# Two levels of a gated recurrence: the same score blocks from narrower matmuls

## The reference, cut to what matters

```
def step(state, xs):
    qc, kc, vc, gc = xs
    cum = jnp.cumsum(gc, axis=2)
    o_inter = jnp.einsum('bhtk,bhkv->bhtv', qc * jnp.exp(cum), state)
    rel = jnp.where(tri[:, :, None], cum[:, :, :, None, :] - cum[:, :, None, :, :], -jnp.inf)
    scores = jnp.einsum('bhtk,bhsk,bhtsk->bhts', qc, kc, jnp.exp(rel))
    o_intra = jnp.einsum('bhts,bhsv->bhtv', scores, vc)
    ...
```

## Time and profile before

| | |
|---|---|
| median of 3 runs | 2507.85 us (2505.35 to 2508.05) |
| the profiled execution, its own time | 2508.06 us |
| its span, first to last instruction | 2506.3 us |
| mean granted TensorE clock | 0.994 |
| TensorE matmul busy | 2473.7 us, 99% |
| TensorE weight loads busy | 2067.1 us, 82% |
| VectorE busy | 1455.4 us, 58% |
| ScalarE busy | 1251.8 us, 50% |

### The profile page before, as it was taken

The page is one execution under the profiler, slowest core; times in us unless marked ns, Lnnn a source line. Parts: engine busy times, 40 slices in busy tenths (PEclk is TensorE's granted clock), DMA queues, the critical chain, the costliest instruction groups (busy, mean ns, idle before and its releaser), DMA issues.

```text
span 2506.3 us, 32631 instructions
## 1 busy us (share of the span) xinstructions
PE 2473.7 (99%) x11947; PEld 2067.1 (82%) x11947; DVE 1455.4 (58%) x1732; ACT 1251.8 (50%) x1604; POOL 44.9 (2%) x103
## 2 busy tenths in 40 slices
PE   8999999999999999999999999999999999999997
PEld 7888878888888888888888888878888888888886
DVE  6479665545445454445566566566666666544465
ACT  5357744444444444444654355456556555444464
POOL 2300000000000000000000000000000000000000
PEclk9999999999999999999999999999999999999999
DMA  7543445666666666555654555555565656665554
GB/s 254 175 134 113 135 136 184 191 187 191 186 191 188 189 192 202 192 192 178 171 175 135 151 143 177 186 158 183 186 185 183 190 178 189 199 200 193 193 194 142
DMA packets 234754, 446.27 MB, mean 178 GB/s; under 512 B 14288, under 2 KB 31012, under 8 KB 234144
## 3 DMA queue, kind: packets, MB, share of 16 engines
q1 hardware_dynamic: 231920, 434.83, 56.2%
q0 software_dynamic: 2736, 10.10, 1.3%
HBM read 442.78 MB, written 2.10 MB: 178 GB/s over the span
## 4 chain that ended last, share of the span: by engine, by line
PE 96%; DVE 2%; ACT 1%; issue 0%; DMA 0%; SPq 0%; DVEq 0%; ACTq 0%
PE pg L2191 26%; PE pg L2193 26%; PE pg L2192 26%; PE pg L2250 3%; PE pg L2251 3%; PE pg L2252 3%; PE pt L2851 1%; DVE wlo L1347 1%; PE pt L2666 1%; PE pt L2262 1%; PE pt L2370 1%; PE pt L2435 1%; PE pt L2461 1%; PE pt L2448 0%; PE pt L2649 0%
## 5 line engine op out<-in xcount | busy, mean ns | idle before, releaser
L1347 DVE TENSOR_TENSOR wlo<-raw,whi 128x1024 fp32r<-128x1024 f32 (+3 forms) x844 | 1004.9, 1197 | 980.4 <-ACT whi L653 978.7
L653 ACT ACTIVATE whi<-raw 128x1024 fp32r<-128x1024 f32 (+3 forms) x844 | 871.8, 1036 | 1164.1 <-PE pg L2193 1048.5
L2191 PE MATMUL pg<-whi,AH 128*128 128x512 f32 (+1 forms) x1920 | 749.5, 390 | 5.1 <-DVE AL L1486 3.0
L2193 PE MATMUL pg<-whi,AL 128*128 128x512 f32 (+1 forms) x1920 | 742.8, 387 | 0.0
L2192 PE MATMUL pg<-wlo,AH 128*128 128x512 f32 (+1 forms) x1920 | 742.1, 387 | 0.0
L2191 PEld LDWEIGHTS pg<-whi,AH 128*128 128x128 f32 x1920 | 362.1, 189 | 77.1 <-DVE AL L1486 3.4
L2193 PEld LDWEIGHTS pg<-whi,AL 128*128 128x128 f32 x1920 | 361.6, 188 | 73.7
L2192 PEld LDWEIGHTS pg<-wlo,AH 128*128 128x128 f32 x1920 | 362.3, 189 | 70.8
L2191 PE MATMUL pg<-whi,FH 128*128 128x512 f32 x696 | 271.3, 390 | 0.0
L2193 PE MATMUL pg<-whi,FL 128*128 128x512 f32 x696 | 270.8, 389 | 0.0
L2192 PE MATMUL pg<-wlo,FH 128*128 128x512 f32 x696 | 270.8, 389 | 0.0
(11 more groups left out here) (477 smaller groups left out, 2033.1 us busy)
## 6 DMA issues: line engine op xcount, KB each, us to landing
raw<-w_up SPq DMA_DIRECT2D x264, 512.0 KB, 3.8
raw<-w_down SPq DMA_DIRECT2D x176, 512.0 KB, 3.6
raw<-w_in SPq DMA_DIRECT2D x152, 512.0 KB, 3.6
raw<-w_gate SPq DMA_DIRECT2D x88, 512.0 KB, 3.6
raw<-w_out SPq DMA_DIRECT2D x64, 512.0 KB, 3.6
raw<-w_ple_gate SPq DMA_DIRECT2D x32, 512.0 KB, 4.5
raw<-w_in SPq DMA_DIRECT2D x32, 388.0 KB, 3.2
raw<-w_in SPq DMA_DIRECT2D x16, 280.0 KB, 3.0
```

Source lines behind the costliest of these rows:

```text
L653: A(whi[:, n % RING, 0:w], raw[:, n % RING, 0:w], ACT.Copy).then_inc(hi_ready, 1)
L1347: V.tensor_tensor(wlo[:, n % RING, 0:w], raw[:, n % RING, 0:w], whi[:, n % RING, 0:w].bitcast(F32), ALU.subtract).then_inc(lo_ready, 1)
L2191: mm(o, xh, wh, start=first and k == 0, stop=False)
L2193: ins = mm(o, xl, wh, start=False, stop=last and k == SK - 1)
```

## The change

`lv_level` gets a branch for l of 1 and 2. In place of one matmul with 128 keys (stationary) and 64 queries (moving) for each token block and head, it issues one for each group of 2b tokens, with the b keys of the first half and the b queries of the second half. For the level of 64 that is one matmul of 64 keys by 64 queries. For the level of 32 it is two of 32 keys by 32 queries, with outputs at partitions 0 to 31 and 64 to 95. The contraction stays 128 features long. The other levels, all other engines and all waits are the same.

```
--- before.py
+++ after.py
@@ -2843,6 +2843,16 @@
                 if l == 0:
                     for h in range(8):
                         ins = mm(head_place(0, h), LG[0][:, 0, h * P:(h + 1) * P], LG[0][:, 1, h * P:(h + 1) * P], start=True, stop=True)
+                elif l <= 2:
+                    b = LEVELS[l - 1]
+                    for t in range(NT):
+                        for h in range(8):
+                            g = LG[l % 2][:, t, h * P:(h + 1) * P]
+                            o = pt[:, lv_bank(l) + t, h * 64:(h + 1) * 64]
+                            for m in range(64 // b):
+                                k0 = 2 * b * m
+                                ins = mm(o[k0:k0 + b, b * m:b * (m + 1)], g[:, k0:k0 + b], g[:, k0 + b:k0 + 2 * b],
+                                         start=True, stop=True)
                 else:
                     b = LEVELS[l - 1]
                     for t in range(NT):
```

## The result

The changed kernel takes 2498.71 us (median of 9 runs, 2496.96 to 2501.36). The kernel before, run beside it, takes 2505.41 us (9 runs, 2502.68 to 2508.35). The ratio is 0.9974 with a 95% interval of 0.9964 to 0.9984: faster by 6.7 us, where 2.9 were forecast, and outside the range of 2501.0 to 2508.3. The profiled execution took 2498.37 us, 9.7 us less than the profiled one of before.

What follows compares the result with a forecast made beforehand. TensorE's matmul stream was taken to bound the kernel. From the profiled 2508.06 us, 1.45 us saved at each of the levels of 64 and 32, 2.9 in all, gave 2505.2 us, range 2501.0 to 2508.3.

Steps and rivals of the forecast that it cites:

- TensorE as the bound: Whole kernel: TensorE's matmul side is busy 99% of the span, so time saved there counts unless a wait swallows it.
- the gain kept through the wait: Wait at the level of 32: its chain starts after the shortened block, so it stays 1.57 us and 1.45 is kept.
- Level of 64: Block of the level of 64: 32 passes at 0.056 us plus 0.35 instead of 3.59 us, saving 1.45 us.
- The price at the edge: At each narrow block's edges: changing the tiling mode drains the engine, taken as 0.35 us for each level.
- Level of 32, in single file: Block of the level of 32: 64 passes one after another at 0.028 us, 1.79 plus 0.35, saving 1.45 us.
- my lower bound: Block of the level of 32: passes run two at a time, 32 x 0.028 + 0.35 = 1.25 us, a gain of 2.3.
- the clock falls as before: Forecast case at the level of 32: both blocks shrink, the granted clock still falls; 2505.2 us, chance 0.45.
- the case in which it stays up: Rival at the level of 32: denser passes keep the clock up, 3.4 us more saved, 2501.8 us, chance 0.28.
- The starting point: Base of the sum: the profiled execution's 2508.06 us; the median of the runs, 0.2 below, was let go.
- The issue bound: Rival at the level of 32: 64 passes at about 0.06 us each cost 4.2 us; 2507.2 us, chance 0.18.
- The constant price of 0.112: Rival at both levels: a pass costs about 0.112 us whatever its width; 2512.3 us, slower, chance 0.06.
- the swallowed gain: Rival: the wait at the level of 32 swallows the gain of the level of 64; 2506.7 us, chance 0.03.

Runs made afterwards that it cites:

- the single-file one: Changed kernel, but at the level of 32 all matmuls of the first output half are issued before the second half: 2499.42 us, ratio 0.9976 to the kernel before.
- the last kernel: Changed kernel plus levels of 16 and below and the diagonal in four matmuls each, TensorE's hooks of levels 128 and 32 one step later: 2482.07 us, ratio 0.9907.

## Why the prediction was wrong

- **TensorE as the bound, and the gain kept through the wait: right.** The wait is 1.57 us in both traces and its chain moved up with the shortened block.
- **Level of 64: right.** Forecast 1.79 + 0.35 = 2.14 us, measured 2.21; 1.38 us saved where 1.45 were forecast. A pass takes (2.08 - 0.27)/31 = 0.058 us, where 0.27 is what one such pass lasts, so the rate of 0.875 ns a column from the earlier trace rows held to 4%.
- **The price at the edge: right** at 0.35 us a block; 2.21 less 32 passes at 0.058 leaves 0.35.
- **Level of 32, in single file: this step failed.** "I take 0.028 in single file: the loads of rows 8 may or may not have overlapped" gave 2.14 us; the block costs 1.26, my lower bound (1.25) to 0.01. Passes whose outputs alternate between partitions 0 and 64 run two at a time, loads included: undoing the alternation (2.16 us) and adding it at the level of 64 (1.28 instead of 2.21) settle it. The earlier trace rows had said so for moving sides of 256 columns, and between two ends I took the cautious one; it cost 0.9 us.
- **The clock at the level of 32: this step failed too, and it is the larger one.** The forecast had "the clock falls as before" (0.45), with 0.28 for the case in which it stays up. The measured case is that one; a clock of 1.00 from 1325 to 1340 us was named as a sign of being wrong, and it came. It stays up in the profiles of the changed kernel, of the one with only the level of 32 narrow, of the single-file one and of the one with 128 moving columns, and the last shows that the block need not get shorter: 3.2 us by its median. One fall costs 3.2 us by the timeline. That a narrow pass fills a quarter of the array was set against this case; the single-file kernel fills a quarter of the columns as well and had no fall in 7 of 11 runs. With the pairs and the clock the forecast would have been 2505.2 - 0.9 - 3.4 = 2500.9, still above the median of 2498.7.
- **The starting point.** The sum was made from the profiled execution, 2508.06 us, and I set its difference to the median of three runs aside. That execution holds a fall of the clock at line 2546 too, worth some 3 us, which not every run has; the median of the nine runs is 2505.41, 2.6 us lower. This covers the rest of the miss (2.2 us), and is no part of the change. The same trace held the sign of it, a clock of 0.50 from 340 to 345 us, and the forecast left it out.
- **The rivals.** The issue bound of 0.06 us a matmul did not show: 64 passes in 1.13 us are 0.018 each, and 128 of them 0.0094. The 0.06 of the earlier trace rows was no issue pace: the same prediction takes those passes as pairs at 0.109 us, 0.054 each. The Trainium skill, TensorE: Matmul & The Clock Gate, in the section "Wait — 56ns, not 53.3ns?", gives about 62 ns a matmul for a setting with hardware decode off. This trace does not show such a floor (64 passes in 1.13 us), and no run here shows which setting it had. The constant price of 0.112 is out, and so is the swallowed gain.
- **Pairs and the skill.** The rows above agree with the Trainium skill, TensorEngine Tiling (Array Packing), Key Properties: different tiles can load weights and multiply in parallel.

## What to carry to other kernels

A float32 matmul with no more moving columns than stationary ones was paid here by its stationary columns; cut it to the rows of the output that are read, and order the pieces so that neighbours write to different 32- or 64-partition places. Each block of such pieces costs some 0.35 us at its edges, which the gain has to cover. Where TensorE waited and then ran passes of 128 by 64, the halved clock cost 3.2 us, twice the wait of 1.57: look at the granted clock behind every wait, and try other work in the wait or other passes behind it. Before summing from one profiled execution, see how its own time stands among the runs and where in it the clock was low.

## What I had not expected of the hardware

- Four float32 passes of 32 stationary and 16 moving columns, with outputs at partitions 0, 32, 64 and 96, go in little more than the time of one: 128 passes in 1.20 us, where 32 passes of 32 by 32 in single file take about 1.0.
- Doubling the moving columns of a block made the median 3.2 us lower (ratio 0.9989), at the same pace of passes: 10 of 11 runs had no fall of the clock, where 5 of 33 had none before.
- One fall of the clock cost 3.2 us at the level of 32 and as much at line 2546, and by their mean clocks some runs of a kernel have it and others not: the 33 runs of the kernel before in one batch spread from 2502.55 to 2508.64 us, the 4 of the last kernel over 0.4 us.
